# A transformer stack on one core: the forget gate's arithmetic, the table that interleaves the scans, and when a late share of the modulation is summed

## The reference

```python
mod = silu(c) @ ada_w + ada_b                        # 6 vectors of 1024: sh_m, sc_m, gt_m, sh_f, sc_f, gt_f
h = rms_norm(x, norm_mix_g) * (1 + sc_m) + sh_m
proj = h @ w_in                                      # queries, keys, values, gates of three mixers
o_a = mixer_diff_attn(...)                           # softmax attention, difference of two maps, 4 heads
o_b = mixer_hgrn2(...)                               # gated recurrence, both directions
o_c = mixer_gla(...)                                 # gated recurrence, both directions
merged = g_a * (o_a @ w_up_a) + g_b * (o_b @ w_up_b) + g_c * (o_c @ w_up_c)
x = x + gt_m * (merged @ w_out)
h = rms_norm(x, norm_mlp_g) * (1 + sc_f) + sh_f
x = x + gt_f * (square(relu(h @ mlp_w1)) @ mlp_w2)
```

```python
log_f = log_sigmoid(z) + log1p(lb * exp(minimum(-z, 80)))
k     = (1 - lb) * sigmoid(-z)
```

## Time and profile before

| What | us |
|---|---|
| median of 3 runs | 2213.25 |
| all runs | 2214.77, 2213.0, 2213.25 |
| the profiled execution's own time | 2214.77 |
| its span in the profile | 2213.0 |
| busy: PE | 2181.9 (99%) |
| busy: DVE | 1110.5 (50%) |
| busy: POOL | 1062.9 (48%) |
| busy: ACT | 878.1 (40%) |
| mean granted TensorE clock | 0.997 of full speed |

### The profile page before, as it was taken

One profiled execution on the slowest core, in us unless ns is written; L12 is line 12 of the kernel. 1 busy time (PEld: TensorE's weight loads), 2 busy tenths in 40 slices (PEclk: granted clock), 3 DMA queues, 4 the chain that ended last, 5 costly groups with the idle time before them and its releaser, 6 DMA issues.

```text
span 2213.0 us, 28784 instructions
## 1 busy us (share of the span) xinstructions
PE 2181.9 (99%) x11670; PEld 1820.9 (82%) x11670; DVE 1110.5 (50%) x1695; ACT 878.1 (40%) x1666; POOL 1062.9 (48%) x810
## 2 busy tenths in 40 slices
PE   7999999999999999999999999999999999999998
PEld 4888777879888888888888888888888888888887
DVE  4776577387612214485752434611644447625253
ACT  4555544354322324475432322533323335322234
POOL 2655454455544446435354545444534454544444
PEclk9999999999999999999999999999999999999999
DMA  7221225574322222312132232233222231232321
GB/s 311 77 77 58 67 88 183 192 281 161 132 97 98 93 97 94 98 59 85 69 112 98 76 115 95 79 117 107 80 95 77 96 104 68 95 109 87 102 103 58
DMA packets 41251, 237.27 MB, mean 107 GB/s; under 512 B 4640, under 2 KB 6816, under 8 KB 15776
## 3 DMA queue, kind: packets, MB, share of 16 engines
q1 hardware_dynamic: 39760, 232.67, 29.8%
q10 hardware_dynamic: 1360, 2.78, 0.4%
HBM read 225.99 MB, written 8.39 MB: 106 GB/s over the span
## 4 chain that ended last, share of the span: by engine, by line
PE 90%; DVE 5%; ACT 2%; POOL 1%; issue 1%; DMA 1%; SPq 0%; DVEq 0%; POOLq 0%; ACTq 0%
PE PS L755 89%; POOL WL L2667 1%; DVE HLO L1919 1%; PE PS L1202 1%; DVE PS L1919 1%; DVE X L1913 1%; DMA RAW<-in_wts 1%; DVE VV L1916 0%; DVE DD L1913 0%; PE PS L1084 0%; ACT WH L1353 0%; ACT T L1478 0%; DVE PS L1913 0%; DVE Y L1913 0%; DMA GT<-spill 0%
## 5 line engine op out<-in xcount | busy, mean ns | idle before, releaser
L2667 POOL TENSOR_TENSOR WL<-RAW,WH 128x512 fp32r<-128x512 f32 (+1 forms) x688 | 918.3, 1363 | 1033.3 <-ACT WH L1353 1012.4
L755 PE MATMUL PS<-HHI,WH 128*128 128x512 f32 x1488 | 593.2, 399 | 0.3 <-DVE HLO L1919 0.3
L755 PE MATMUL PS<-HLO,WH 128*128 128x512 f32 x1488 | 580.1, 390 | 0.0
L755 PE MATMUL PS<-HHI,WL 128*128 128x512 f32 x1488 | 580.0, 390 | 0.0
L1353 ACT ACTIVATE WH<-RAW 128x512 fp32r<-128x512 f32 (+1 forms) x688 | 378.7, 613 | 413.9 <-PE PS L755 380.5
L755 PEld LDWEIGHTS PS<-HHI,WH 128*128 128x128 f32 x1488 | 279.7, 188 | 73.4 <-issue 14.1
L755 PEld LDWEIGHTS PS<-HHI,WL 128*128 128x128 f32 x1488 | 279.6, 188 | 59.2
L755 PEld LDWEIGHTS PS<-HLO,WH 128*128 128x128 f32 x1488 | 279.9, 188 | 57.2 <-issue 2.6
L755 PE MATMUL PS<-UF,WH 128*128 128x512 f32 (+1 forms) x832 | 223.9, 357 | 0.0
L1913 DVE TENSOR_TENSOR T<-PS,R 128x512 f32<-128x512 f32 x112 | 76.9, 690 | 215.3 <-PE PS L755 209.9
L755 PEld LDWEIGHTS PS<-UF,WH 128*128 128x128 f32 x832 | 148.3, 189 | 22.6
(11 more groups left out here) (347 smaller groups left out, 3206.3 us busy)
## 6 DMA issues: line engine op xcount, KB each, us to landing
RAW<-in_wts SPq DMA_DIRECT2D x182, 1024.0 KB, 4.8
LX<-in_wts SPq DMA_DIRECT2D x8, 1024.0 KB, 5.0
FW<-in_wts SPq DMA_DIRECT2D x6, 1024.0 KB, 12.3
spill<-T SPq DMA_DIRECT2D x24, 256.0 KB, 5.0
RAW<-in_wts SPq DMA_DIRECT2D x8, 768.0 KB, 4.2
GT<-spill SPq DMA_DIRECT2D x20, 256.0 KB, 4.9
X<-in_xt SPq DMA_DIRECT2D x2, 1024.0 KB, 6.9
out_x<-X SPq DMA_DIRECT2D x8, 256.0 KB, 2.3
```

The costliest lines, as they stand in the source:

```text
L755: return e.matmul(o_, l, r, start=start, stop=stop)
L2667: return e.tensor_tensor(o_, a, b, f)
```

## The change

Four things change.

1. The forget gate. DVE now makes `TB = min(-z, 80)` and, waiting for it, `TC = max(TB - 40, 0)`; POOL has a step of its own at n = 3, `TB = TB - TC` of 128x1024, which waits for TC and gives the event that ACT's exp(TB) waits for. ACT's addition of 40 is gone, its exp(TC) has the scale -1, since TC now has the other sign, and DVE's n = 4 adds TC and waits for one event fewer. It holds for both directions.
2. The table in line 25 has new numbers for DECAY, for the first pair of RECUR and for ATTEND.
3. In `out`, the four parts of `shares(5, 1)` are all summed behind the second group of residual additions. Before, two stood there and two between the takes of the tail.
4. In `boundary`, `later_mod(5)` and AF stand ahead of `add(0, 3)` and `take(1, 0)`. A constant of 40 is no longer set.

```diff
@@ -22,7 +22,7 @@
 DENSE = [("cv", 0), ("bz", 0), ("bz", 1), ("cg", 0), ("bq", 0), ("bv", 0), ("av", 0), ("aq", 0), ("ak", 0), ("av", 1), ("aq", 1), ("ak", 1),
          ("bg", 0)] + [("gate", n) for n in range(12)]
 NATURAL = ("cv", "bv", "av")
-DECAY, RECUR, ATTEND = ((15, 2.2), (34, 2.3)), ((8, 1.15), (65, 2.2)), (73.5, 1.65)
+DECAY, RECUR, ATTEND = ((16, 2), (34, 2.2)), ((8, 1.1), (65, 2.2)), (75, 1.7)
 LEVELS = [(r, lv) for r in range(3) for lv in range(8)]
 PAIRS = (2, 1, 1)
 
...
@@ -1569,13 +1569,11 @@
                     table()
                 q.wait_ge(*at(("ea", p)))
                 e.activation(TA, TA, ACT.Ln, bias=1.0).then_inc(*up("a_mix", ("la", p)))
-                q.wait_ge(*at(("cap", p)))
-                e.activation(TC, TC, ACT.Identity, bias=EPSC[:, 4:5]).then_inc(*up("a_mix", ("excess", p)))
             elif n == 4:
                 q.wait_ge(*at(("uc", p)))
                 e.activation(TB, TB, ACT.Exp).then_inc(*up("a_mix", ("eu", p)))
                 q.wait_ge(*at(("lsc", p)))
-                e.activation(TC, TC, ACT.Exp).then_inc(*up("a_mix", ("ec", p)))
+                e.activation(TC, TC, ACT.Exp, scale=-1.0).then_inc(*up("a_mix", ("ec", p)))
                 q.wait_ge(*at(("lk", p)))
                 e.activation(K_, K_, ACT.Exp, scale=-1.0).then_inc(*up("a_mix", ("sg", p)))
             elif n == 5:
...
@@ -2021,16 +2019,14 @@
 
             for p in range(4):
                 take(0, p)
-                if p < 2 and n == "out":
-                    ada(5, 1, p + 2)
                 if p > 1:
                     add(0, p - 1)
-            add(0, 3)
-            take(1, 0)
             if n == "out":
                 later_mod(5)
                 q.wait_ge(*at(("later_mod", 5)))
                 stt(AF[:, :], MOD[:, 32:40], 1.0, v("gmlp", 0, 8), ADD, MUL).then_inc(*up("d_mix", ("af",)))
+            add(0, 3)
+            take(1, 0)
             if nx is None:
                 take(1, 1)
                 product(0, 2, 4, ("x_post", "sgu", 7, 1))
...
@@ -2171,8 +2166,9 @@
             if n == 2:
                 q.wait_ge(*at(("ev", U["bz", p], 1)))
                 q.wait_ge(*at(("zc", 1) if p == 0 else ("log_b", 0)))
-                ts(TB, Z, -1.0, 40.0, MUL, MIN).then_inc(*up("d_mix", ("uc", p)))
-                ts(TC, Z, -80.0, -40.0, MAX, MIN).then_inc(*up("d_mix", ("cap", p)))
+                ts(TB, Z, -1.0, 80.0, MUL, MIN).then_inc(*up("d_mix", ("u", p)))
+                q.wait_ge(*at(("u", p)))
+                ts(TC, TB, -40.0, 0.0, ADD, MAX).then_inc(*up("d_mix", ("cap", p)))
             elif n == 3:
                 q.wait_ge(*at(("la", p)))
                 stt(K_, Z, 0.0, TA, MAX, ADD).then_inc(*up("d_mix", ("lk", p)))
...
@@ -2180,8 +2176,7 @@
                 stt(Z, Z, 0.0, TA, MIN, SUB).then_inc(*up("d_mix", ("ls", p)))
             elif n == 4:
                 q.wait_ge(*at(("ls", p)))
-                q.wait_ge(*at(("excess", p)))
-                tt(Z, Z, TC, SUB).then_inc(*up("d_mix", ("lsc", p)))
+                tt(Z, Z, TC, ADD).then_inc(*up("d_mix", ("lsc", p)))
             elif n == 5:
                 q.wait_ge(*at(("eu", p)))
                 q.wait_ge(*at(("ec", p)))
...
@@ -2392,10 +2387,7 @@
                 q.wait_ge(*at(("x_again", k)))
                 q.wait_ge(*at(("later_mod", 1)))
                 stt(X[:, k, :], PS[:, BANK[i, m], :], MOD[:, 16 + k:17 + k], X[:, k, :], MUL, ADD).then_inc(*up("d_ev", ("ev", i, m)))
-            if j == 0:
-                shares(5, 0)
-        ada(5, 1, 0)
-        ada(5, 1, 1)
+            shares(5, j)
         later_mod(4)
         boundary("out")
 
...
@@ -2726,6 +2718,11 @@
         split_after(U["cqk", 0])
         split_after(U["lr", 0])
 
+        def decay(p, n):
+            if n == 3:
+                q.wait_ge(*at(("cap", p)))
+                tt(G3[1][:, :, :], G3[1][:, :, :], G3[2][:, :, :], SUB).then_inc(*up("p_mix", ("uc", p)))
+
         def differ(r, lv):
             m, g, D = 64 >> lv, 8 * r + lv, level(r, lv)[:, :, :]
             sums = Am[:, :].rearrange("p (i t) -> p i t", i=2)[:, :, 0:512]
...
@@ -2759,6 +2756,8 @@
         for step, *a in P.steps:
             if step == "split":
                 split(*a)
+            elif step == "decay":
+                decay(*a)
             elif step == "differ":
                 differ(*a)
             elif step in ("reach_k", "reach_q"):
...
```

More of the change, by code:

```diff
@@ L456, in build @@
     LB = place("LB", o, [24]); o += 96
-    EPSC = place("EPSC", o, [5]); o += 32
+    EPSC = place("EPSC", o, [4]); o += 32
     GF = place("GF", o, [8]); o += 32
@@ L2079, in vector_program @@
         e.memset(EPSC[:, 3:4], 1.0 / 32)
-        e.memset(EPSC[:, 4:5], 40.0)
         e.memset(EPSC[:, 1:2], EPS * EPS).then_inc(*up("d_norm", ("eps",)))
```

## The result

| | us |
|---|---|
| changed kernel, median of 4 runs | 2225.48 (2225.22 to 2227.62) |
| kernel before, median of 4 runs beside it | 2214.01 (2213.0 to 2215.72) |
| ratio | 1.0052, 95% interval 1.0039 to 1.0065 |
| profiled execution of the changed kernel | 2227.24, span 2224.9 |

The account below looks back on a forecast made before the run. PE was taken as the bound, busy 2181.9 of 2213.0 us, so only its waits count. Terms sum to +5.65 us: profiled 2214.77 becomes 2220.4, less 1.52 for the median gives 2218.9; range 2213.0 to 2223.9.

Parts of the forecast that it names:

- First gate and first levels: First forget gate: products want their banks sooner and DVE gets later, so PE waits, +4.2 us (1.2 to 5.4).
- Product of level 4: Product at 121.92: shorter lead for ACT's KN nearly cancelled by PE's late arrival, +0.2 us (-0.1 to +0.7).
- Carry: Product at 134.08, now directly behind the state: nothing hides DVE's carry, +1.35 us (+1.3 to +2.3).
- Second half: Second half of the recurrences: attention steps fall behind KN, removing PE's waits for KN and SB, -1.8 us (-2.0 to -0.3).
- End of `out`: Two more parts of the share stand ahead of the tail's first take, so PE waits, +1.7 us (+0.3 to +2.6).
- Rival B: First gate: DVE's lateness runs on, first term 7 to 8 us, +10.7 us or 2223.9 in all; chance 0.14.
- Rival A: DVE between 87 and 93 us keeps pace, losing nothing to POOL: +1.5 us or 2214.8 in all; chance 0.30.
- rival C: Whole kernel: the table's reordering removes more small waits than counted, -5.4 us or 2207.9; chance 0.06.
- the pair at 80.68: Two DVE instructions (G from ZB), 3.40 us beside POOL against 1.29 at 117.57: 2.1 us lost.

Follow-up runs that it names:

- gate_only: The kernel before with the change's forget gate alone (POOL's subtraction, no ACT addition): 2217.25 us against 2214.98, ratio 1.0014.
- attend_only: The kernel before with ATTEND = (75, 1.7) alone: 2214.58 us against 2214.45, ratio 0.9998.
- table_only: The kernel before with line 25 of the change alone: 2219.40 us against 2214.98, ratio 1.0020.

## Why the prediction was wrong

By its own steps:

- **First gate and first levels, +4.2.** The mechanism was right and the size near: 3.2 us of waits for a collect (0.7 and 2.5). POOL's subtraction took 3.37, in the forecast's 2.6 to 3.9 (`gate_only` has one of 2.37, so 2.6 was no lower bound), and DVE's gap was 1.21. Not priced was ACT's queue behind exp(TB). What the step missed is the 3.3 us at the lower clock behind the 2.47 us wait.
- **Product of level 4, +0.2.** No wait there of that kind was seen. Right, and worth nothing.
- **Carry, +1.35.** It was 1.48, and 1.6 more of low clock behind it.
- **Second half, -1.8.** This term failed on its own. The wait for KN went in the changed kernel, but the one of 0.2 for SB stayed and two came, of 0.6 for the eviction T and 0.4 for DVE's T, so PE waits 0.6 less. Even so, from 147 to 430 us, where the two orders differ and can be compared only roughly, the changed kernel loses about 0.7 us where it should have gained. That is in PE's busy time at the full clock, and its cause stays open. `attend_only` shows the exchange by itself: ratio 0.9998. The step that failed is the cover that the shift costs: the prediction looked for it at a collect (up to 1.5 us) and not at the projection's eviction, which ACT does in the same order.
- **End of `out`, +1.7.** It was 2.01, and 1.7 more of low clock.
- **The sum.** The waits in the terms come to 3.2 + 1.5 + 2.0 = 6.7 against 7.25 forecast. What the sum left out is that PE's busy time is no constant: 6.6 us at half speed behind the three waits. Rival B, "the lateness runs on", gave 2223.9 and comes nearer, but by luck: it gave the first term 7 to 8 us of waits, and 3.2 were seen. Rival A, that DVE keeps pace, is refuted by DVE's 2.0 us lost beside the subtraction and by the 2.0 us of waits for a collect in `gate_only`; rival C, that the table wins, by `table_only`.

Two readings in the prediction were off without moving its sum. POOL's 1.95 us at 89.76 ends before the collect at 92.19 begins, so neither of the two collects that speak for rival A ran beside it. And the pair at 80.68, which it takes as bearing out a rule on DVE's instructions with two inputs in SBUF, has one such input each.

The clue stood in the profile of before. Its granted clock is 0.997, and the view by stretch for the start shows 0.79 behind PE's waits there. I read the clock only in the two stretches where PE never waited, and both show 1.00.

The measured total is then as follows. At 60 us the changed kernel is 1.8 us ahead, because the profiled execution of before had two low stretches there and it had none. From there to 441 us, where both kernels have the same order again, it loses 9.7 us. The waits for the two collects and the carry (4.7) and the low clock behind them (4.9) are 9.6 of this, so all other shifts together, the second half's among them, come to nothing. The end of `out` adds 3.7 and small waits elsewhere 0.3: 11.9 us, as between the spans. Taken over runs, it is less clean, since a low stretch comes or stays away from run to run. The one execution in ten of the changed kernel with a mean clock of 0.999 took 2220.39 us, 7.1 above the 2213.25 that the prediction started from and near the 6.7 of the waits alone; the other nine lie between 2225.2 and 2227.8.

## What to carry to other kernels

Where PE is busy nearly all the time, a wait of one to two microseconds is to be priced at its length and, in part of the executions, 1.7 us more for the stretch at 1.2 GHz behind it. Behind 60 us no wait under 1.1 us had such a stretch behind it; ahead of 60 us one of 0.82 had it in 7 of 15 traces, so short waits are safer and not safe. Cut the largest waits first, and rather leave three of 0.7 us than one of 2. Filling a wait of 2.0 us with 1.8 us of work that isn't needed cost nothing measurable here. An engine's step that is moved is to be followed in the queue of every engine that walks the same list, above all ACT, where a quarter of a weight that waits for its DMA holds up whatever stands behind it.

## What was not expected of the hardware

Over the fifteen traces, behind 60 us, the waits of PE were followed by this:

| length of the wait | waits | a stretch at 1.2 GHz behind |
|---|---|---|
| 2.0 to 3.9 us | 10 | 9 |
| 1.35 to 1.6 us | 20 | 4 |
| 1.1 to 1.25 us | 6 | 1 |
| 0.5 us to under 1.1 | 92 | 0 |

The first 60 us are different. All fifteen traces have the wait of 0.82 us near 49, and in 7 of them a low stretch begins 1.5 to 2.4 us behind its end; in 7 there is one near 23 us, behind waits of at most 1.0 us. So the length of the last wait does not decide it alone.

Behind 60 us, the wait for KN, 1.56 us, never had one, in eight traces; the wait of 1.6 for a collect had one in both traces that have it, and the one of 1.43 to 1.48 for the carry in two of four. No low stretch there lacks a wait of 1.1 us or more ahead of it, but for the one at the end of the program, which begins behind PE's last matmul. One stretch costs 1.6 to 1.7 us each time, and behind two of the waits of 2.5 it was two lengths in one, 3.3 to 3.4 us. What makes the difference among the middle ones stays open.

A GpSimd subtraction of 128x1024 took 2.37 to 3.38 us, and VectorE's instruction beside it 3.28 in place of 1.23: the two ran one after the other and not side by side, as the Trainium skill has it ("SBUF — State Buffer", "Who interferes with whom"). VectorE's instruction started at 85.58 and ended at 88.86, 1.08 us behind the end of POOL's at 87.78, and it took 1.23 in the kernel before. The 3.37 us of POOL's fit this too: it began at 84.41 while VectorE's QKB ran, which ended at 85.54, and from there it is 2.24 us to 87.78, near the shortest length of 2.37.
